# A kernel that gathers 128 rows beside its matmuls: the share of gathered rows laid on its middle stage goes from 0.8 to 0.5

## The reference

```python
top_s, pos = lax.top_k(cand_s, PEER_TOPK)          # 16 of 256 candidates
idx = jnp.take_along_axis(cand_i, pos, axis=-1)    # (128 tokens, 8 heads, 16)
gate = jax.nn.softmax(top_s, axis=-1)
u = expert_u[idx]
v = expert_v[idx]
act = jax.nn.gelu(jnp.einsum("thkd,td->thk", u, xt))
return jnp.einsum("thk,thkd->td", (gate * act).astype(v.dtype), v)
```

## Time and profile before

| what | value |
|---|---|
| median of 3 runs | 3920.38 us (3919.8 to 3929.22) |
| the profiled execution, device time | 3918.28 us |
| its span in the profile | 3916.5 us |
| late stage, from its first panel on PE | 854.84 to 930.12 us |
| parked stage | 930.12 to 1362.38 us |
| expert stage | 1362.38 to 1658.15 us |

### The profile page before, as it was taken

How to read it: one execution, slowest core, us unless ns; L and a number is a source line. 1 busy time by engine, 2 the same in 40 slices (tenths; PEclk the granted TensorE clock), 3 DMA queues, 4 the chain that set the end, 5 groups by cost and what they waited for, 6 DMA issues and landing times. The chain is left out here.

```text
span 3916.5 us, 50618 instructions
## 1 busy us (share of the span) xinstructions
PE 3636.3 (93%) x17238; PEld 3073.9 (78%) x17238; DVE 2128.2 (54%) x3409; ACT 1503.4 (38%) x2617; POOL 1920.9 (49%) x1478
## 2 busy tenths in 40 slices
PE   7979998988999999999988989999759999889999
PEld 6457998978999999888867747888647887667887
DVE  7782997866999777643234444332233322554320
ACT  3433555743333343544323334332214432443431
POOL 4623675436788777555423414544325544114544
PEclk9989999989999999999999979999979999899999
DMA  3012453668999899432332202223593333012232
GB/s 128 22 65 75 155 169 131 226 262 319 385 404 408 330 347 354 155 97 96 95 114 68 81 6 76 95 92 93 63 78 97 97 96 115 25 33 88 94 93 90
DMA packets 173478, 569.83 MB, mean 145 GB/s; under 512 B 15377, under 2 KB 59025, under 8 KB 155828
## 3 DMA queue, kind: packets, MB, share of 16 engines
q1 hardware_dynamic: 153972, 430.30, 32.6%
q0 software_dynamic: 19392, 138.16, 11.6%
HBM read 518.33 MB, written 50.07 MB: 145 GB/s over the span
## 5 line engine op out<-in xcount | busy, mean ns | idle before, releaser
L277 POOL TENSOR_TENSOR weight_low<-weight_ring,weight_high 128x512 fp32r<-128x512 f32 x1264 | 1723.5, 1385 | 1836.6 <-ACT weight_high L249 1430.8
L291 PE MATMUL banks<-normed_high,weight_high 128*128 128x512 f32 (+1 forms) x2528 | 951.4, 376 | 38.7 <-ACT weight_high L249 22.6
L249 ACT ACTIVATE weight_high<-weight_ring 128x512 fp32r<-128x512 f32 x632 | 399.0, 631 | 1440.8 <-PE banks L298 1283.2
L292 PE MATMUL banks<-normed_low,weight_high 128*128 128x512 f32 (+1 forms) x2528 | 941.6, 372 | 0.0
L298 PE MATMUL banks<-normed_high,weight_low 128*128 128x512 f32 (+1 forms) x2528 | 573.8, 368 | 5.9 <-POOL weight_low L277 5.7
L291 PEld LDWEIGHTS banks<-normed_high,weight_high 128*128 128x128 f32 x2528 | 484.5, 192 | 111.5 <-issue 38.0
L292 PEld LDWEIGHTS banks<-normed_low,weight_high 128*128 128x128 f32 x2528 | 484.2, 192 | 61.8 <-issue 2.0
L298 PEld LDWEIGHTS banks<-normed_high,weight_low 128*128 128x128 f32 x2528 | 462.2, 188 | 68.4 <-POOL weight_low L277 9.3
L251 ACT ACTIVATE weight_high<-weight_ring 128x512 fp32r<-128x512 f32 (+1 forms) x632 | 389.8, 617 | 90.1 <-PE banks L298 80.6
L2037 DVE TENSOR_TENSOR square<-square,banks 128x512 f32<-128x512 f32 x88 | 60.5, 688 | 416.0 <-PE banks L298 414.4
L291 PE MATMUL banks<-parked_high,weight_high 128*128 128x384 f32 x768 | 262.4, 342 | 15.9 <-ACT weight_high L249 10.4
(11 more groups left out here) (371 smaller groups left out, 5642.2 us busy)
## 6 DMA issues: line engine op xcount, KB each, us to landing
weight_ring<-in_experts SPq DMA_DIRECT2D x256, 512.0 KB
weight_ring<-in_ffn_gate SPq DMA_DIRECT2D x88, 512.0 KB
weight_ring<-in_ffn_up SPq DMA_DIRECT2D x88, 512.0 KB
weight_ring<-in_ffn_down SPq DMA_DIRECT2D x64, 512.0 KB
expert_gates<-spread_space SPq DMA_DIRECT2D x6, 4096.0 KB, 12.3
parked_space<-expert_gates SPq DMA_DIRECT2D x24, 768.0 KB
parked_space<-parked_activations SPq DMA_DIRECT2D x24, 768.0 KB
weight_ring<-in_a_w_in SPq DMA_DIRECT2D x28, 512.0 KB
```

The source lines that it names most:

```text
L249: m.nc.scalar.activation(m.w_hi[:, s % PARTS, 0:HALF], m.ring[:, s, 0:HALF], ACT.Copy).then_inc(m.half_high, 1)
L277: m.nc.gpsimd.tensor_tensor(m.w_lo[:, s % PARTS, at], m.ring[:, s, at], m.w_hi[:, s % PARTS, at].bitcast(FP), ALU.subtract).then_inc(done, 1)
L291: m.nc.tensor.matmul(out, w_hi, hi(c), start=(first and c == 0), stop=False)
L292: m.nc.tensor.matmul(out, w_hi, lo(c), start=False, stop=False)
```

## The change

One number is different. Everything that is computed stays the same, and so do PE's and SP's instructions and their order.

```diff
 FIRST_DOT = 5
 LAST_DOT = LAST_GROUP_STEP - 2
-PARKED_SHARE = 0.8
+PARKED_SHARE = 0.5
```

## The result

The changed kernel takes 3988.36 us in the median (3981.86 to 3997.56, 4 runs) against 3920.19 us before (4 runs): 1.8% slower, ratio 1.0178 with a 95% interval of 1.016 to 1.0195. The profiled execution took 3981.86 us, with a span of 3980.1 us, 63.6 us longer than before. The direction was forecast; the size was not: 3947 us was predicted, and 3968 us was the top of the range.

A forecast was written before the change was run, and what follows sets the result against it. PE, busy 93% of the span, was taken to bound the kernel, with rows already binding it in places in the expert stage. 0 + 18 + 3 + 3 + 3 = +27 us on 3918.3 gave 3945, as median 3947 us; range 3927 to 3968.

The forecast's parts named there:

- no gain in the steady parked stage: Parked stage from step 25: PE already runs without waits, so taking rows out gains 0.
- the late stage and the first parked steps: Steps up to 24: later rows delay the next group's fetch, partly offset by lost waits; +3 us, between -5 and +8.
- the tail: Steps 158 to 160: two dots and two adds, one more landing before PE needs the sum; +3 us, between 0 and +7.
- the bytes: Expert stage, steps 112 to 159: 11 more fetches, 11.5 MB, at 372 GB/s; +18 us, bounds +7 and +33.
- the term for pairs: Expert stage: two fetches in one step queue behind each other; +3 us beyond what the bytes already cost.
- the third rival above: The last of three rivals listed, the same as the much slower rival; upper bound for the term for pairs.
- the much slower rival: Expert stage: rounds bind, each pair adds a whole landing, 5.57 us a step, +44; total +50, 3970 us; chance 0.13.
- The signs: Parked panels 4.22 us apart, share under 1.00; expert panels 4.9 us; POOL waiting for adds; step 16 gates about 950.
- The ones for the bytes: Expert stage: 360 to 375 GB/s, and DVE's wait for landing rows up from 29.8 us to over 60.

The follow-up runs named there:

- the first experiment: Kernel before with only the late stage's dots as in the changed kernel (14 late, 69 parked, 45 expert): 3932.91 us, ratio 1.003.
- The fourth experiment: Changed kernel with seven row buffers instead of four in the expert stage, so fetches there move earlier: 3927.11 us, ratio 1.0016.
- eleventh: Kernel before with 11 late, 60 parked and 57 expert dots, and seven row buffers in the expert stage: 3917.95 us, ratio 0.9998.
- The third experiment: Kernel before, row schedule unchanged, with 24 added transfers of 0.49 MB on SP's queue in the expert stage: 3926.64 us, ratio 1.0018.
- the seventh: Kernel before with seven row buffers instead of four in the expert stage: 3906.30 us, ratio 0.9971.
- fifth: Changed kernel with every add one step after its dot instead of two: 3928.84 us, ratio 1.0037.
- ninth: Kernel before with 47 expert dots, exactly one in each step from 112 to 158, late dots unchanged: 3924.02 us, ratio 1.0023.
- the twelfth experiment: Kernel before with seven row buffers in the expert stage and 7 late, 72 parked, 49 expert dots: 3913.36 us, ratio 0.9993.

## Why the prediction was right and wrong

**Right: no gain in the steady parked stage.** PE is busy for all of the 364.10 us from step 25 on, 4.23 us a panel, with the DMA share down from 1.00 to 0.94. The rows taken out gave nothing back, as forecast.

**Right: the late stage and the first parked steps, a little small.** +3 was taken, +6.4 came, within -5 to +8; the first experiment shows it alone. Its working held in outline. DVE's first gates of step 16 started at 952.67 (forecast: about 950), 5.4 us later than in the earlier trace rows where 3 was forecast. PE at step 19 got its high parts and then waited for POOL:

```profile
957.99 0.97 PE L298 MATMUL banks<-parked_high,weight_low 128*128 128x384 f32 x4 [3.70 <-POOL weight_low L277]
...
964.95 0.66 PE L291 MATMUL banks<-parked_high,weight_high 128*128 128x384 f32 x1 [4.07 <-ACT weight_high L249]
```

**Right in number only: the tail**, +2.9 against +3. The reason given for it was two dots and two adds behind one more landing. The fourth and eleventh experiments have the same dots and adds there, and their steps 160 to 175 take 78.5 us against 78.4 before. The 2.9 us came with the long rounds, so this match was luck.

**Near in size, but not what binds: the bytes.** I took +18 from the rate at the end of the late stage. The third experiment measures +9.4 for bytes alone, and the fourth and eleventh, with all that comes with the 57 rows, +15.0 and +14.7 against the seventh with its 45. These two moved 401 and 406 GB/s. The 372 GB/s that I chose was no ceiling, though it was read at a share of 0.99: in these traces a DMA share of 0.99 to 1.00 goes with 372, 390, 401 and 406 GB/s, so a full share alone doesn't tell what rate can be had. The rule of the Trainium skill that I weighed, about 358 GB/s on the HBM side ("DMA: Bandwidth & Descriptors", "Where 436 GB/s comes from"), is contradicted further by these two.

**Wrong: the term for pairs.** This is the step that failed: "I add +3 for what isn't, bounded by 0 below and by the third rival above." In its place the runs show 48 us: the 63.1 us of the stage less the 15.0 that the same rows cost with seven buffers. (The fourth experiment is 58.8 us shorter than the changed kernel, but 10.7 us of this seven buffers give the kernel before as well.) It is not the pairs as such that cost it, since the fourth and fifth experiments have all ten of them, but the wait for a free buffer, a wait that the sum did not have. I had read the round from the earlier trace rows, 13.9 us for three steps, and had written its consequence down as the much slower rival with 5.57 us a step and +44 in the stage; then I gave it 0.13 and argued against it that the landing time was mostly queueing and would shrink. It shrank by little: where DVE had to wait for a row, the median from the start of its issue to its dot went from 8.1 to 7.6 us, the DMA share fell to 0.85, and the stage still took 5.84 us a step. With 1.2 rows a step and four buffers, 35 of the 57 rows are fetched into a buffer that is freed in the step just before their own dot (before, always two or three steps ahead), so the landing is in series with POOL, DVE and ACT. From the start of its issue to the end of its add a row held its buffer for 19.7 us in the mean (17.8 before). 57 x 19.7 / 4 = 281 us, and the stage took 280.5: all four buffers were in use nearly all the time. Before, 45 x 17.8 / 4 = 200 of 217 us. I treated bytes and round as the same time counted twice. They are two different limits, and the slower one sets the pace.

**Too small even in the rival.** The rival's +44 was 5.57 us a step where 5.84 came. It spoke of the clock but had no term for it, and 24.7 us of the 63.1 are matmuls that ran longer. It also left out the gate multiplies beside POOL.

**The signs.** Of those named, the spacing at 4.22 us in the parked stage and POOL waiting for adds came. The ones for the bytes did not: 308 GB/s instead of 360 to 375, and 48.1 us of waits for landing rows instead of over 60.

**The range.** It reached "just short of the middle" of the much slower case. With the round read from rows, and nothing but an argument against it, that case should have had the larger chance.

## What to carry to other kernels

Free bandwidth is one limit on the requests that fit into a time slot, and buffers are another: (buffers) divided by (time from the fetch to the release of its buffer) must exceed the rate, and the landing, every engine in between and every fixed distance in the schedule count in that time. Here 4 / 19.7 us is one row in 4.9 us, where 1.2 rows in 4.22 us were asked for. Before moving gathers to where the DMA has room, look at how many steps of lead the fetches have there; at lead 0 add buffers first or release them sooner. In the kernel before, 34 of the 45 rows already had lead 0; at one row a step that cost 11 us (217.4 against 206.7), and 1.2 rows a step made it 59. And a wait in one engine's queue (here POOL's for a buffer) that also makes something for the critical engine turns a late fetch into a late matmul.

## What was not expected of the hardware

The untouched rest of the program, after step 175, took 2258.3 us in the profile of before and 2248.4 in that of after, with identical instructions. Windows of 300 us at the same distance from step 175, before (first) and after, show a granted clock of 0.89 and 0.94:

```profile
2150.00:2450.00 300.00, 279.80 (x1078) 195.78 (x1077) 147.10 (x214) 113.67 (x222) 95.48 (x72) 0.89 0.18 56
```

```profile
2223.60:2523.60 300.00, 279.39 (x1131) 201.13 (x1130) 151.77 (x220) 118.51 (x228) 102.10 (x77) 0.94 0.19 60
```

Over the 14 profiles this rest took 2248.4 to 2261.1 us, at mean granted clocks from 0.954 (2249.0 us) down to 0.947 (2261.1 us). So some 13 us of this kind can stand between any two executions, and single profiles must be compared by stage.

The parked stage is nearer to an edge than its clean 4.22 us a panel let me think. At 0.75 rows a step DVE is busy for 95% of it. At 0.82 rows it lost 33 us, with adds a step earlier 29 us, and in the profiles of the first and ninth experiments, with 69 and 70 rows evenly spread, 18 and 9 us, each time with PE waiting for `parked_low`; at 60 rows it took 370 us. The loss is not gradual: most groups of 8 panels keep their 33.7 us, and single ones take 35 to 41. DVE's load alone doesn't explain it, since the twelfth experiment, with 72 rows evenly spread, took 374.7 us, only 1 more than before. The cause stays open.
